# Norms, turning, first projection pass and wo by blocks of 128 tokens, and grouped rows, in a four-layer diffusion trunk

## The reference

```python
def modulate(x, g, shift, scale):
    return rmsnorm(x, g) * (1 + scale) + shift
...
    for i in range(DEPTH):
        ...
        hc = modulate(xc, norm_mix[i], sh1c, sc1c)
        hl = modulate(xl, norm_mix[i], sh1l, sc1l)
        ...
        xc = xc + g1c * oc
        xl = xl + g1l * ol
        hc = modulate(xc, norm_ffn[i], sh2c, sc2c)
        hl = modulate(xl, norm_ffn[i], sh2l, sc2l)
        xc = xc + g2c * moe(hc, w_router, router_bias, moe_w_gate[i], moe_w_up[i], moe_w_down[i])
        xl = xl + g2l * moe(hl, w_router, router_bias, moe_w_gate[i], moe_w_up[i], moe_w_down[i])
    y_prompt = rmsnorm(xc, final_norm)
    y_sample = rmsnorm(xl, final_norm)
```

## Time and profile before

| | |
|---|---|
| median of 3 runs | 1791.16 us (1788.07 to 1794.7) |
| the profiled execution | 1796.09 us |
| its span in the trace | 1794.2 us |
| PE busy | 1456.9 us, 81% of the span |
| DVE, ACT, POOL busy | 505.7, 371.0, 186.3 us |
| HBM traffic | mean 242 GB/s over the span |

### The profile page before, as it was taken

One profiled execution on the slowest core, in us unless ns is written; L12 is line 12 of the kernel. 1 busy time (PEld: TensorE's weight loads), 2 busy tenths in 40 slices (PEclk: granted clock), 3 DMA queues, 4 the chain that ended last, 5 costly groups with the idle time before them and its releaser, 6 DMA issues.

```text
span 1794.2 us, 25885 instructions
## 1 busy us (share of the span) xinstructions
PE 1456.9 (81%) x10581; PEld 893.4 (50%) x10581; DVE 505.7 (28%) x1227; ACT 371.0 (21%) x951; POOL 186.3 (10%) x258
## 2 busy tenths in 40 slices
PE   2999987997598897998398989789875998969970
PEld 1776675332376685332184456653323876853320
DVE  0226423110335514111313342321104255141103
ACT  1106320110213601111110342201102045011111
POOL 1000011000222021000201000110001010110001
PEclk9899998999699998999689999889996999979985
DMA  9796325999975044799949103259998730538983
GB/s 344 272 359 168 118 71 196 417 422 418 339 239 148 1 176 171 304 422 421 356 175 270 52 9 141 71 223 418 421 418 311 241 54 1 217 138 317 422 334 109
DMA packets 126192, 435.35 MB, mean 243 GB/s; under 512 B 12611, under 2 KB 54550, under 8 KB 101494
## 3 DMA queue, kind: packets, MB, share of 16 engines
q1 hardware_dynamic: 96854, 350.32, 50.6%
q0 software_dynamic: 22272, 79.47, 12.9%
q10 hardware_dynamic: 6944, 3.84, 0.7%
HBM read 389.15 MB, written 44.45 MB: 242 GB/s over the span
## 4 chain that ended last, share of the span: by engine, by line
PE 72%; DMA 10%; DVE 7%; issue 5%; ACT 3%; POOL 1%; SPq 1%; POOLq 0%; DVEq 0%; ACTq 0%
PE bank L1468 63%; DMA work<-in_moe_w_gate 3%; PE bank L1618 3%; PE bank L1524 2%; DMA xn<-y_slots,row_of 2%; DMA y_slots<-kT 2%; PE bank L1765 1%; DMA ring<-in_w_mod 1%; DMA V<-in_moe_w_gate 1%; DVE xn L1043 1%; ACT pp L925 1%; DVE V L1445 1%; DVE V L1447 1%; DVE x L1448 1%; POOL small L616 1%
## 5 line engine op out<-in xcount | busy, mean ns | idle before, releaser
L1468 PE MATMUL bank<-ring,pp 128*32 128x512 f32 x2168 | 409.8, 605 | 37.0 <-issue 33.9
L1468 PE MATMUL bank<-ring,hT 128*128 128x256 f32 (+3 forms) x1142 | 262.9, 391 | 6.8 <-DVE hT L1054 4.2
L1468 PEld LDWEIGHTS bank<-ring,hT 128*128 128x128 f32 x1142 | 209.8, 192 | 58.9 <-issue 26.2
L1468 PE MATMUL bank<-work,pp 128*32 128x512 f32 x888 | 232.7, 620 | 1.7 <-DVE pp L1384 1.0
L1468 PEld LDWEIGHTS bank<-ring,pp 128*32 128x32 f32 x2168 | 108.6, 111 | 217.4 <-issue 213.1
L1468 PE MATMUL bank<-ring,xn 128*128 128x256 f32 x768 | 166.8, 380 | 0.0
L1468 PE MATMUL bank<-V,pp 128*32 128x512 f32 x784 | 153.2, 611 | 3.2 <-DVE pp L1384 3.2
L1468 PEld LDWEIGHTS bank<-ring,xn 128*128 128x128 f32 x768 | 145.6, 190 | 19.8
L1468 PE MATMUL bank<-ring,condT 128*32 128x256 f32 x1536 | 116.2, 432 | 38.2 <-DMA ring<-in_w_mod 30.4
L1400 DVE TENSOR_TENSOR pp<-bank,pp 128x256 f32<-128x256 f32 x40 | 17.0, 425 | 350.1 <-ACT pp L997 350.1
L1468 PEld LDWEIGHTS bank<-ring,condT 128*32 128x32 f32 x1536 | 53.5, 122 | 96.8 <-DMA ring<-in_w_mod 40.3
(11 more groups left out here) (225 smaller groups left out, 1521.5 us busy)
## 6 DMA issues: line engine op xcount, KB each, us to landing
ring<-in_w_mod SPq DMA_DIRECT2D x96, 1024.0 KB, 8.7
ring<-in_moe_w_down SPq DMA_DIRECT2D x52, 1024.0 KB, 19.7
ring<-in_moe_w_gate SPq DMA_DIRECT2D x29, 1024.0 KB, 13.7
ring<-in_moe_w_up SPq DMA_DIRECT2D x29, 1024.0 KB, 16.2
y_slots<-kT POOLq DMA_DIRECT2D x40, 512.0 KB, 8.4
V<-in_moe_w_gate SPq DMA_DIRECT2D x19, 1024.0 KB, 13.4
V<-in_moe_w_up SPq DMA_DIRECT2D x19, 1024.0 KB, 16.3
hT<-h_slots POOLq DMA_DIRECT2D x36, 512.0 KB, 11.8
```

The source lines that it names most:

```text
L1468: return pe.matmul(out, lhsT, rhs, start=start, stop=stop)
```

## The change

The work around each norm is cut into blocks of tokens. Layer openings follow `opening(L)`: block 0 is normed, turned and projected with two units, then block 1 is turned, two more units of block 0, then block 2 is turned, the last two units of block 0, and a second pass projects blocks 1 and 2 with all units. DVE puts the combination of token block 2 behind the read-out of block 0's norm. wo runs block by block, and the norms of blocks 0 and 1 are turned between its projections. The router has two jobs. `hrow` writes the features in groups (feature 8p + k goes to place 128k + p), so that the gather, the turning and the rows in HBM read contiguous pieces. The scaled rows of the second norm lie in `kT` and in the scratch `squares`. The ring is planned with `unit_ends`, written-out estimates of when each unit is done; all units of the first pass are fetched ahead of the mods that follow them.

```diff
+def opening(L):
+    steps = []
+    for b in range(NB):
+        steps += [("norm", b)] + [("unit", u) for u in projections(L)[2 * b:2 * b + 2]]
+    return steps
...
 def layer_units(L):
-    mods = mod_units(L)
-    units = list(mods["first"])
-    for name, u in mixer_units(L):
+    mods, opened = mod_units(L), opened_units(L)
+    units = list(mods["first"]) + [(name, L, u) for name, u in opened]
+    for key in opened:
+        units += mods.get(key, [])
+    for name, u in mixer_units(L)[len(opened):]:
         units += [(name, L, u)] + mods.get((name, u), [])
...
+        order += [((part, L, u, b), alt[b % 2]) for u in projections(L) for b in (1, 2)]
...
+def unit_ends():
...
+        for u in range(4):
+            ends["wo", L, u] = now + 27.0 + 3.4 * (u + 1)
+        now = pass_mods(mods["route"], now + 65.0) + 12.0
+        for e in range(E):
+            ends["moe_g", L, e] = ends["moe_u", L, e] = now + 12.0 * last_block(e) + 7.0
+            ends["moe_d", L, e] = now + 12.0 * last_block(e) + 23.0
...
+    def take(key, slot):
+        place[key] = (slot, fills[slot])
+        fills[slot] += 1
+        free_at[slot] = ends[key]
...
             elif name == "moe_g":
                 pair = min(GATE_UP, key=lambda p: max(free_at[p[0]], free_at[p[1]]))
                 for part, slot in zip(("moe_g", "moe_u"), pair):
-                    take((part, L, e), slot, now + 1 + 4 * last_block(e))
+                    take((part, L, e), slot)
...
             if key[0] == "hrow":
-                return xn[:, key[2], key[3] * 512:(key[3] + 1) * 512], ps[:, :]
+                rows = xn[:, key[2], :].rearrange("p (k c j) -> p c j k", k=KC, c=KC)
+                return rows[:, 4 * key[3]:4 * key[3] + 4], ps[:, :].rearrange("p (c j k) -> p c j k", c=4, k=KC)
@@ POOL @@
+            def norm_power(n, b):
+                pool.wait_ge(sumsq, 3 * n + b + 1)
+                rms_power(small[:, b:b + 1], small[:, 4 + b:5 + b], D, rstd_ready)
@@ ACT @@
-                norm_in(2 * L, L, False)
+                norm_in(2 * L, 0)
                 mods_out(mods["first"])
-                norm_out(2 * L, 0)
+                norm_in(2 * L, 1)
+                for what, at in opening(L):
+                    if what == "unit":
+                        evacuate((part, L, at, 0))
+                        continue
+                    norm_out(2 * L, at)
+                    if at == 0:
+                        norm_in(2 * L, 2)
@@ DVE @@
+            def combine(L, b):
+                dve.wait_ge(y_scaled, 3 * L + b + 1)
...
+                norm_scale(2 * L, 0)
+                for n, (what, at) in enumerate(opening(L)):
+                    if what == "norm":
+                        norm_out(2 * L, at)
+                        if at == 0 and L > 0:
+                            combine(L - 1, 2)
+                    elif mine((part, L, at, 0), "v"):
+                        evacuate((part, L, at, 0))
+                    if what == "unit" and n % 3 == 1 and n < 6:
+                        norm_scale(2 * L, n // 3 + 1)
                     for i, u in enumerate(QKV_ORDER):
-                        evacuate(*[("qkv", L, u, b) for b in range(NB)])
+                        evacuate(*[("qkv", L, u, b) for b in (1, 2)])
                         if i > 0:
                             if kind == 1:
                                 normalise(i - 1, QKV_ORDER[i - 1])
                             turn_heads(i - 1, QKV_ORDER[i - 1])
...
-            norm_scale(2 * DEPTH)
-            dve.wait_ge(xn_ready, 3 * (2 * DEPTH + 1))
             for b in range(NB):
-                last = V_.tensor_tensor(xn[:, b, :], xn[:, b, :], gbc[:, 0, 0, :], ALU.mult)
+                dve.wait_ge(rstd_ready, 3 * 2 * DEPTH + b + 1)
+                V_.scalar_tensor_tensor(out=xn[:, b, :], in0=x[:, b, :], scalar=small[:, 4 + b:5 + b],
+                                        in1=gbc[:, 0, 0, :], op0=ALU.mult, op1=ALU.mult).then_inc(xn_ready, 1)
@@ PE @@
-                for u in range(4):
-                    wait_unit(("wo", L, u))
-                    for b in range(NB):
+                for b in range(NB):
+                    for u in range(4):
+                        if b == 0:
+                            wait_unit(("wo", L, u))
+                        if u == 3 and b > 0:
+                            norm_turn(2 * L + 1, b - 1)
                         project(("wo", L, u, b), ("wo", L, u), oT, KC, UC)
-                norm_turn(2 * L + 1)
+                turned_norm(2 * L + 1, 0, 1)
+                router(0, 0, 2 * P)
                 hrow(0)
+                hrow(1)
+                norm_turn(2 * L + 1, 2)
+                turned_norm(2 * L + 1, 2)
+                router(1, 2 * P, P)
...
                         for b in range(NB):
-                            ins = mm(bank[6 + k // 4][:, k % 4 * P:(k % 4 + 1) * P], xn[:, b, k::KC],
+                            ins = mm(bank[6 + k // 4][:, k % 4 * P:(k % 4 + 1) * P], xn[:, b, k * P:(k + 1) * P],
                                      first_of[:, b, :], b == 0, b == NB - 1)
```

284 lines of the change are left out of this document (163 added, 121 removed).

## The result

The changed kernel takes **1758.9 us** (median of 4 runs, 1756.5 to 1761.9) where the kernel before takes 1791.9 (1788.1 to 1794.7): ratio **0.9817, interval 0.9803 to 0.983**. The sign of the forecast was right, its size was not: 33 us in place of 56, and the time lies just outside the range (1710 to 1758).

The account below looks back on a forecast made before the run. TensorE was busy 1456.9 of 1794.2 us, so gains lay in its waits and slow matmuls. Openings 9, wo to rows 18.4, gather 22, experts' stage 1 and end 5.5 sum to 56: 1735 us, range 1710 to 1758.

Parts of the forecast that it names:

- Together 9 us: Layer openings: starting projections once block 0 is normed wins 9 us over four layers (0 to 15).
- the openings do nothing: Rival, openings: a second-pass w_mod unit waiting for a slot, or ACT's mods, takes the gain twice over; 1753 us, chance 0.12.
- the term for the lower clock: Layer openings: TensorE leaves its idle time at the lower clock, costing 1 us in layer 0, 0.8 elsewhere.
- The rival built on it: First pass of the openings: TensorE stays at 1.2 GHz throughout, costing 83 us; 1818 us, chance 0.03.
- Layer 1: Opening of layer 1: DVE's serial heads' norm bounds the second pass, transposes start at 562.2, so -0.9 us won.
- From wo to the rows: Last wo projection to the experts' rows: shorter norm, turning and router path wins 4.6 us a layer, 18.4 in all.
- The gather: Gather of expert block 0: contiguous operands win 6.2 us in layers 0 to 2 and 3.4 in layer 3, 22 in all.
- the gather is swallowed: Rival, experts' stage: block 8 comes at its time whatever block 0 does, losing 22 us; 1757 us, chance 0.13.
- hrow copies above 1 us: Sign of being wrong: copies writing the normed rows take over 1 us each.
- the 3 MB head start: Experts' stage: fetching expert 3 ahead in layers 0 to 2 wins 0.4 us each, 1 us in all.
- its rival of 23 us: Experts' stage: if block 8 is bound by bytes alone, 3 MB win 8 us in three layers; 1712 us, chance 0.1.
- The end: Latent output at the kernel's end: one step for scaling and gain, and a transfer half as long, win 5.5 us.

Follow-up runs that it names:

- 1791 sets: Sets of runs in which the kernel before took 1785 to 1796 us; in the other sets it took 1773 to 1779.
- d_grouped_again: Second run of the kernel before with only the normed rows kept grouped by feature and read contiguously: 1773.9 us, ratio 0.9915.
- d_grouped_alone: First run of the kernel before with only the normed rows kept grouped by feature and read contiguously: 1788.0 us, ratio 1.0063.

## Why the prediction was wrong

**The failed step: "Together 9 us"**, the openings. Worked out layer by layer it costed PE, ACT and DVE and took "the mods" as staying as they are, so that no transfer was waited for in the second pass. In its place the openings lost 16.5 us. Of the 25.5 us between -9 and +16.5:
- 21 are the gate's broadcast (569.3 to 548.3 with one wait moved back; 18 to 22 in the ratios). The step did not ask what else hangs on "block 0 of unit 5 is read out". The change moves that event from the end of the projections to the middle, and with it POOL's queue; it is POOL's transfers, not PE's order, that the w_mod units then met. The rival "the openings do nothing" named the stall (a w_mod unit of the second pass) but as a wait for a slot, and priced it at 18 us; releasing the slots earlier gives 3 at most. It was the right place and the wrong mechanism, and that its 1753 us is near the measured time is luck.
- 4 to 5 remain, and much of it is the term for the lower clock, which was mis-sized. It stood at 1 us in layer 0 and 0.8 elsewhere; the first pair of projections shows 1.5, 2.9 and 2.3 us in layers 0, 1 and 3 (8.53, 10.00 and 9.39 for 7.07). In layer 1, 2.1 us over its forecast, projections start 0.9 us earlier than forecast, the clock takes 2.1 more than it was given, and the second pass and the way from the transposes to the scores are 0.6 longer each, which nearly adds up. Layer 2 is 2.6 over; its units have unequal widths, and I did not part it further.

The Trainium skill (TensorE: Matmul & The Clock Gate, Part 1) has the clock fall when the engine idles; the trace agrees that it is down after 8.12 us of idle time, though it had been at half since about 444, well before that gap. The rival built on it, that the whole first pass runs at half the clock, did not occur: the third and fourth projections take 7.07. The cost in the sum was taken from a rise 5.5 us after the turning began, in which PE had 24 turns without a break; with 8 turns, a gap and then projections it came after 9.4.

**Layer 1** was right in its mechanism, read from the earlier trace rows: DVE bound, the start of the second pass 0.9 us off when counted from block 9, its length 0.6 us.

**From wo to the rows** was right and small: 22.6 for 18.4. **The gather** was right: 5.62 us in layers 0 to 2 (forecast 5.5) and 7.37 in layer 3 (forecast 8), 21.4 for 22 in the stretch, although layer 2 gives back 4 of it to rows that come late. That it is passed on was right in the 1791 sets only, and that the first comparison fell into one was luck. The rival "the gather is swallowed" had its chance of 0.13 and describes the other sets; its text said "no row here says how early they are", and that was the row to look for. The Trainium skill's rule on 16-byte lines (SBUF — State Buffer, "Door 1: The DMA port swizzle"), taken in the forecast for the writes as well, is borne out on that side: the copies take 1.03 and 1.04 us for 0.69 and 0.59, one of the signs of being wrong that the forecast named ("hrow copies above 1 us"). In the old order that costs 1.2 us a layer, near the 6 in all that I kept as an upper bound while the sum took 0; in the new order it is hidden.

The experts' stage, read from the earlier trace rows as one of fixed length, kept it (94.4 to 95.4 us from block 0's first product to block 8, forecast 94.5): **the 3 MB head start** gave nothing (428.3 for 428.1, forecast 1 us less), and its rival of 23 us is refuted. **The end** was 6.8 for 5.5. In the sum itself the four layers of the openings give 8.5, not 9, and "slower" has 0.03 in one place and 0.04 in another; neither matters.

## What to carry to other kernels

When work is split into passes, list every wait on an event that the split moves, on the queues too, and follow each one: here a single wait of POOL on "block 0 of the last unit" moved 1 MB of broadcast into the busiest stretch and cost 21 us, two fifths of the 51 gained at the other places. Whatever a faster step releases sooner (slots, and so weights) may overtake the transfer that the next step waits for, as the two traces of grouped rows suggest; look at the distance between the two issues (here 3.3 us behind in one trace and 0.7 ahead in the other), and try to hold the one that can wait, which was not tried here where it would matter. And cut both traces into stretches that belong to one part of the change each: the sum of the differences then accounts for the whole time, and one row shows where to look. Last, compare only runs made side by side, and more than once: one edit of the kernel before gave 0.9915 in one set and 1.0063 in another.

## What the runs showed of the hardware

- A broadcast of 1 MB from HBM to 128 partitions (1 KB pieces by the kernel's layout) on POOL's queue: with 0.26 MB of state outputs it took 38% of the sixteen DMA engines over 30 us for 1.31 MB, and the window fell to 132 GB/s at a share of 0.95, against 229 at 0.65 in the same stretch without it and 346 at 0.94 behind that. A 1 MB unit beside it landed after 13.4 us instead of 5.3. The same loads with slack around them cost nothing (1.0007), though there too the units landed later (10.3 us for 7.2). Whether the small pieces, the repeated reading of one source or the queue makes it slow, no run tells.
- TensorE's stream of matmuls pauses by itself in some sets of runs (gates to gather 17.1 to 19.9 us) and not in others (12.6 to 14.2), with the DMA engines equally full. The same kernel has the pauses in one set and not in another (`d_grouped_again` and `d_grouped_alone`); it would be 12 of the 15 us by which the kernel before moves. The ratio of one and the same edit changed its side of 1 between the two: 0.9915 and 1.0063.
- PSUM read-outs of 128x512 that write one element every 512 bytes: 1.03 us on DVE (0.69 contiguous), 1.04 on ACT (0.59).
- In the opening of layer 1 the granted clock stayed at 0.5 (1.2 GHz) through 8.12 us of idle time, 8 turns, the wait for their read-out and the start of the projections, and rose 9.4 us after the turning began; before, after 14.95 us of idle time, it rose 5.5 us after it, with 24 turns in one piece.
